# A fused two-block transformer kernel on one core: the context tokens loaded later, and normalised and transposed behind the first key/value product of x

## What is computed

```python
h = rmsnorm(x, g_pre_mix) * (1 + sc1) + sh1                    # x: 256 tokens
h_ctx = rmsnorm(ctx, g_pre_mix) * (1 + mod_c[1]) + mod_c[0]    # ctx: 256 tokens
# sh1, sc1, ... = silu(c) @ w_mod + b_mod;  mod_c = silu(c_ctx) @ w_mod[:, :2048] + b_mod[:2048]
k_a, v_a, k_b, v_b, q_a, q_b, g_a, g_b = split_cols(h @ w_in, IN_SPLITS)
parts = split_cols(h_ctx @ w_in[:, :KV_COLS], IN_SPLITS[:4])
```

## Time and profile before

| | |
|---|---|
| time, median of 3 runs | 1680.76 us (1679.63 to 1681.08) |
| the profiled execution's own time | 1681.33 us |
| its span, first to last instruction | 1679.5 us |
| mean granted TensorE clock | 0.996 |
| PE busy | 1636.7 us, 97% of the span |
| PE weight loads | 838.1 us, 50% |
| DVE busy | 585.6 us, 35% |
| ACT busy | 273.1 us, 16% |
| DMA | 528.83 MB, mean 315 GB/s |

### The profile page before, as it was taken

One profiled execution on the slowest core, in us unless ns is written; L12 is line 12 of the kernel. 1 busy time (PEld: TensorE's weight loads), 2 busy tenths in 40 slices (PEclk: granted clock), 3 DMA queues, 4 the chain that ended last, 5 costly groups with the idle time before them and its releaser, 6 DMA issues.

```text
span 1679.5 us, 21504 instructions
## 1 busy us (share of the span) xinstructions
PE 1636.7 (97%) x8226; PEld 838.1 (50%) x8227; DVE 585.6 (35%) x1209; ACT 273.1 (16%) x566; POOL 7.6 (0%) x5
## 2 busy tenths in 40 slices
PE   7999999999999999999999999999999999999998
PEld 4757785433333333332333333333355688599953
DVE  1755432412121212121212122121232623378883
ACT  3114421100000100000001000000131221132211
POOL 0010000000000000000000000000000000000000
PEclk9999999899999999999999999999999999999999
DMA  9687336699999999999999999999983222444420
GB/s 402 261 344 307 133 131 241 251 379 427 427 431 427 428 430 427 430 429 427 430 428 427 430 427 429 429 427 430 428 358 140 111 101 101 166 164 172 153 86 25
DMA packets 38676, 528.83 MB, mean 315 GB/s; under 512 B 4338, under 2 KB 4738, under 8 KB 6370
## 3 DMA queue, kind: packets, MB, share of 16 engines
q1 hardware_dynamic: 36720, 521.16, 74.7%
q10 hardware_dynamic: 1906, 6.97, 1.1%
HBM read 527.05 MB, written 1.06 MB: 314 GB/s over the span
## 4 chain that ended last, share of the span: by engine, by line
PE 75%; DMA 23%; ACT 1%; DVE 1%; issue 0%; SPq 0%; ACTq 0%; DVEq 0%
DMA arena_ring<-experts_dram 22%; PE scores L2263 16%; PE proj L1943 9%; PE att_out L2297 9%; PE proj L1933 7%; PE proj L2526 4%; PE proj L2072 3%; PE proj L2110 3%; PE scores L2581 2%; PE proj L2229 2%; PE scores L2526 2%; PE turned L2218 2%; PE proj L1975 2%; PE scores L2149 1%; PE turned L2581 1%; PE turned L2526 1%
## 5 line engine op out<-in xcount | busy, mean ns | idle before, releaser
L2263 PE MATMUL scores<-arena_ring 128*64 128x512 f32 x2112 | 467.7, 593 | 12.6 <-DMA arena_ring<-experts_dram 12.1
L2263 PEld LDWEIGHTS scores<-arena_ring 128*64 128x64 f32 x2112 | 150.2, 137 | 317.8 <-issue 286.4
L2297 PE MATMUL att_out<-arena_ring 128*64 128x512 f32 x1056 | 242.6, 602 | 0.0
L1524 DVE COPY arena_ring<-turned 128x512 f32<-128x512 f32 x33 | 22.8, 692 | 463.1 <-PE turned L2218 463.1
L1943 PE MATMUL proj<-arena_ring 128*128 128x512 f32 x352 | 155.3, 599 | 2.5 <-DVE arena_ring L1311 2.5
L2297 PEld LDWEIGHTS att_out<-arena_ring 128*64 128x64 f32 x1056 | 70.3, 137 | 147.3 <-issue 121.0
L1933 PE MATMUL proj<-arena_ring 128*128 128x256 f32 x512 | 113.1, 381 | 0.0
L1943 PEld LDWEIGHTS proj<-arena_ring 128*128 128x128 f32 x352 | 66.6, 192 | 83.5 <-issue 80.2
L1933 PEld LDWEIGHTS proj<-arena_ring 128*128 128x128 f32 x512 | 96.5, 190 | 14.9 <-issue 1.8
L920 ACT ACTIVATE arena_ring<-arena_ring 128x512 f32<-128x512 f32 x33 | 20.8, 630 | 475.3 <-DVE arena_ring L1527 475.3
L1431 DVE TENSOR_SCALAR arena_ring<-cst,arena_ring 128x128 f32<-128x128 f32 x68 | 20.5, 344 | 165.6 <-PE turned L2303 165.6
(11 more groups left out here) (418 smaller groups left out, 1457.3 us busy)
## 6 DMA issues: line engine op xcount, KB each, us to landing
arena_ring<-experts_dram SPq DMA_DIRECT2D x192, 2048.0 KB, 26.1
arena_ring<-stream_dram SPq DMA_DIRECT2D x53, 2048.0 KB, 8.7
arena_ring<-stream_dram SPq DMA_DIRECT2D x4, 1024.0 KB, 19.2
arena_ring<-bias_dram ACTq DMA_DIRECT2D x1, 2048.0 KB, 14.1
arena_ring<-gain_rows_dram ACTq DMA_DIRECT2D x3, 512.0 KB, 7.5
xtok<-xtok_dram SPq DMA_DIRECT2D x1, 1024.0 KB, 5.4
arena_ring<-ctxtok_dram SPq DMA_DIRECT2D x1, 1024.0 KB, 7.7
arena_ring<-mod_rows_dram ACTq DMA_DIRECT2D x2, 512.0 KB, 10.5
```

The source lines that it names most:

```text
L2263: ins = mm(AS[n][parts, :], xe[:, k % 4, k // 4, :], weights(s, kk * 2 * D + n * D + feats.start), start=False, stop=k == KD - 1, skip_gro ...
L2297: ins = mm(AO[parts, :], act_s[:, kk, s - 4, :], weights(s, kk * D + feats.start), start=s == 4 and kk == 0, stop=s == 5 and kk == 3)
```

## The change

The context's load is issued after slots 0, 1 and 2 instead of before them. On ACT, its squares and root follow the first four modulated tiles of x instead of the squares of x. On DVE, its normalisation follows the first half of the modulation instead of the normalisation of x. On PE, its sixteen transposes follow the first half of the k_b/v_b product of x instead of standing on both sides of `mod_turn(0)`. The counts that DVE waits for are renumbered to match.

```diff
             sp.dma_start(xtok[:], A["xtok"]).then_inc(x_in, 16)
-            sp.dma_start(ctok, A["ctxtok"]).then_inc(ctx_in, 16)
             for n in range(N1):
+                if n == 3:
+                    sp.dma_start(ctok, A["ctxtok"]).then_inc(ctx_in, 16)
                 load(n)
...
             token_squares(xtok, 0)
-            act.wait_ge(ctx_in, 16)
-            token_squares(ctok, 1)
             for h in range(2):
...
             modulated_x(0)
+            act.wait_ge(ctx_in, 16)
+            token_squares(ctok, 1)
             modulated_x(1)
...
             normed_tokens(xtok, xnorm, 0)
-            dve.wait_ge(ctx_in, 16)
-            normed_tokens(ctok, ctok, 1)
             def context_turned(b):
-                dve.wait_ge(xn_turned, [5, 6, 8, 9][b])
+                dve.wait_ge(xn_turned, 6 + b)
...
-                dve.wait_ge(xn_turned, [7, 10][half])
+                dve.wait_ge(xn_turned, [5, 10][half])
...
+            modulation(0)
+            dve.wait_ge(ctx_in, 16)
+            normed_tokens(ctok, ctok, 1)
             context_turned(0)
             context_turned(1)
-            modulation(0)
             modulated_context(0)
...
             mod_rows_of(0, (0, 1), PB[0])
-            turn_context((0, 1))
             mod_turn(0, PB[1])
-            turn_context((2, 3))
             B[0] = 2
             kv_w, q_w = slot(IN_SLOT[0], KD, 256), slot(IN_SLOT[1], KD, 512)
             need(IN_SLOT[0])
             half_k(PB[2], hT, h_ready, kv_w, 256, 0)
+            turn_context((0, 1, 2, 3))
             half_k(PB[3], hcT, hc_ready, kv_w, 256, 0)
```

## The result

The changed kernel takes 1682.86 us in the median of 17 runs (1680.86 to 1686.06), the kernel before 1680.54 (1674.11 to 1681.50, 17 runs). The ratio is 1.0026 with a 95% interval of 1.0017 to 1.0035: 4.4 us slower, 2.9 to 5.9. The range (1682.6 to 1687.4) held the time, by 0.3 us at its lower end; the forecast median of 1684.9 and the sum's own range (1684.3 to 1685.6) lay above it, and so did the 1684.1 from which the prediction called a time slower, with a chance of 0.70. Both kernels jump between levels, so their medians differ by less (2.3 us) than their ratio says.

The account below looks back on a forecast made before the run. PE, busy 97% of the span, was taken as the bound, so PE's idle time decides. The stage's steps summed to +4.1 us, passed whole to the end: median 1680.76 becomes 1684.9 us, range 1682.6 to 1687.4.

Parts of the forecast that it names:

- The sum for the stage: From first to second modulation rows: second rows start at 37.1 instead of 33.0 us, +4.1 us; chance 0.60.
- step 2: Both transposed context banks taken out ahead of the first modulation: DVE begins at 24.07, not 24.39; gain 0.32 us.
- Step 3: Context's norm after four tiles of x on ACT: PE idles 29.05 to 31.0 before the context's transposes, some 1.9 us.
- Step 4: Context's transposes, DVE's copies and first tile: context's product starts at 33.5 and ends at 37.1 us; PE idles another 0.6.
- step 1: Load order: slots 0, 1, 2 come 1 MB earlier, nobody waits for them; context lands near 20 us, in time; worth 0.
- The clock rival: PE's clock falls in the idle and transposes between 29.05 and 33.5 us: 1.7 us more, 1686.6; chance 0.15.
- Absorbed by the experts: PE's wait for the experts' stream shrinks by its delay: all 4.1 us gone (1680.8) or part (1681 to 1684); chance 0.14.
- Later low stretches: Half-speed clock stretches at 302.5 and 330 us shrink or grow; 1679.9 if both vanish; chance 0.09.

Follow-up runs that it names:

- turn_first: Kernel before with only the modulation rows turned ahead of all context transposes, DVE modulating before it copies the context's banks; 1679.36 us in a single execution.
- pe_order_only: Changed kernel with load, squares and norm of the context back in their old places, only PE's and DVE's order changed; ratio 1.0016 to the kernel before.
- load_only: Kernel before with only the context's load moved behind slots 0, 1 and 2; ratio 1.0027 to the kernel before.
- slot0_halves: Changed kernel with slot 0 loaded by two DMAs of 1 MB instead of one of 2 MB; 1681.53 us in a single run.
- old_load_rest_new: Changed kernel with the context's load back right behind x, the rest still changed; ratio 1.0009 to the kernel before.
- after_again: The changed kernel run once more without any edit; ratio 1.0027 to the kernel before.
- q_first: Changed kernel with the first q_b tile's four products moved ahead of the context's transposes; ratio 1.0031 to the kernel before.
- consts_q_first: Changed kernel with both small constant loads issued by SP ahead of x and the first q_b tile ahead of the context's transposes; ratio 0.9996 to the kernel before.
- consts_first_after: Changed kernel with the two small constant loads issued by SP ahead of x instead of by ACT; ratio 1.0006 to the kernel before.
- pad72: Kernel before with 72 idle transposes on PE ahead of the context's first product; ratio 1.0040 to the kernel before.
- filled: Changed kernel with idle transposes (6, 12 and 14) in PE's three waits around the product of x; 1685.48 us in a single run.

## Why the prediction came out as it did

**The sum for the stage was right.** Predicted +4.1; measured 18.15 - 14.1 = 4.0. By its steps: step 2 gave 0.3 (predicted 0.32; turn_first). Step 3: tile to squares 2.07, squares to inversion 2.54, inversion to transposes 1.67 (2.0, 2.60, 1.67). Step 4: transposes to product 34.02 - 31.53 = 2.49 (2.5). The split into PE's order (2.1) and the late norm (1.9) is confirmed by pe_order_only (2.2 and 1.9).

**The step that failed is step 1, "worth 0".** I asked who waits for the slots and for the context, and never who shares the DMA engines with them. The constants land 2.4 to 2.6 us later, and I had myself written that the start hangs on them and that "none of that is touched". The other half of step 1 held: nobody waited for the slots, and ACT's squares of the context followed its tiles of x without a wait. load_only and slot0_halves show the late constants, the packets show how, and old_load_rest_new puts its price at 2.9 us (0.7 to 5.1). That the whole change still cost 4.4 us, so near the forecast 4.1, is luck: the price that I left out was offset by low-clock time. By the estimate from the granted clocks the changed kernel spends one of its low stretches where it costs nothing and has no more than the kernel before in all (mean clock 0.9968 in after_again, 0.9965 in the kernel before on that chip).

**The clock rival was real, and cheap where I said so.** It fell in seven of the eight profiles in which only four transposes stand between the modulation rows and the product of x (26.6 us in the changed kernel, 26.7, 25.8, 24.0, 26.7, 27.0 and 23.2 in after_again, pe_order_only, old_load_rest_new, slot0_halves, q_first and consts_q_first; not in consts_first_after). I had given it 0.15 with a fall behind the product; it came 0.3 to 0.9 us into the product of x, near the place (25.4 us) for which the prediction put its price at nothing. It was nothing where PE then waited for the late norm, but 1.6 us in pe_order_only and 1.4 in q_first, where no wait followed (in q_first 8.65 us from the product's start to the transposes, against 3.65 + 3.64 at full clock). The statement of the Trainium skill (TensorE: Matmul & The Clock Gate, Part 4: PE-mode transpose) that transposes don't count as busy in the same way isn't borne out by the transposes of this kernel (fp32, listed as MATMUL): pad72 held the clock at 2.4 GHz through 7.86 us of them alone, and filled with transposes alone in the waits. My own argument for it was weaker than it looked: the clock's rise in before is recorded at 19.33 us and so had 0.7 us of products ahead of it, whose first ones ran at the slow pace (the thirty-two took 3.99 us, and 3.64 in the changed kernel). In pe_order_only the rise came at 18.97, behind 3.6 us of transposes and only 0.17 us of products.

**Absorbed by the experts:** no. pad72's delay reached the end (4.2 to 9.2 us by the ratio, 7.7 by the estimate at full clock, of 7.86).

**Later low stretches:** right as a mechanism, wrong in its weight. I read three runs and a profile within 1.7 us as a proof that they don't come and go; 17 runs span 7 us. The profiled execution of the changed kernel ended 0.4 us ahead of before by these: it was 4.73 us late and had three fewer, some 4.8 us.

**What stays open.** At equal clock the changed kernel should lose 4.0 + 2.4 to 2.6 = 6.4 to 6.6 us; the ratio says 4.4 (2.9 to 5.9). The estimate at full clock gives 7.0, give or take 0.9, so the difference lies in low-clock time, as far as a clock recorded to 0.001 and the assumed free stretch carry. Why the low stretches fall where they do, and why the transposes of x run at full pace in seven of the fourteen profiles, no run here shows.

## What to carry to other kernels

A load moved on SP's queue here delayed a small transfer on ACT's queue by 2.4 to 2.6 us, with nobody waiting for the load itself: ask first what the start of the chain waits for, and how large the pieces are that this transfer now lies beside. Work moved behind a product must have all its inputs made before the product ends; here squares and norm, cheap and formerly hidden, came onto the chain because their place on ACT moved too. And where a kernel jumps between levels of several microseconds, measure an edit by the stretch between two fixed instructions and count the low-clock stretches apart, before believing any difference at the end.

## What the runs showed of the hardware

A transfer of 65 KB on ACT's queue took 7.9 to 8.3 us beside loads of 8 KB to a partition on SP's queue, 10.3 to 10.7 us where x was followed by one of 16 KB to a partition, and 1.8 to 2.0 us issued first on SP's queue. Its packets of 520 bytes, eight to a DMA engine, started 0.33 us apart (median) beside the 8 KB pieces and 0.63 beside those of 16 KB.

The low stretches of the clock lasted 3.4 or 6.8 us, each 3.4 costing 1.6 to 1.7 us of a PE-bound stage. In seven of eight profiles one followed a stretch with one short group of four transposes and 2.2 us of waiting; in the one run with these waits filled by transposes there was none, and 72 transposes in a row (7.86 us) ran without a fall.

At the start the granted clock is listed as 1.00 before the first recorded rise, though the matmuls run at half pace (eight transposes in 1.97 us and, after it, in 1.09): the pace of the rows is to be trusted there, not the column.
